# Prompt attention with unscaled probabilities and a token-major value product

## The chip, the cores and the metric

The kernel runs on one core of one Trainium2 chip. The time is that of one execution on the device in microseconds, the median of three runs. The core has five engines with their own instruction queues: TensorE (PE), the vector engine (DVE), ScalarE (ACT), GpSimd (POOL) and SyncE (SP, which here only starts DMAs). They wait for each other with semaphores.

## The reference

One inference step of a decoder layer for a prompt of 512 tokens and 8 sample tokens that each look back on 2048 cached ones. The part that the change touches:

```python
# group A, prompt: 8 heads, causal
s = (q_nope . k_nope + q_rope . k_rope) * MLA_SCALE;  p = softmax(s);  o_mla = p @ v
# group B, prompt: 8 heads, 2 key/value heads; the top-k (128) tokens of an indexer are kept
s = q . k * DSA_SCALE + rel_bias[t5_bucket(distance)];  p = softmax(masked s);  o_dsa = p @ v
# then, for prompt and sample tokens
mix = concat([rms_norm(o_mla, g_a), rms_norm(o_dsa, g_b)], axis=-1)     # each over its 512 columns
x = x + gate_m * (mix @ w_out)
# then norm, SwiGLU feed-forward network, gate, residual
```

All of it is in 32-bit floats.

## The kernel before, in words

Each engine has one program, written out in the order in which it runs. The list `AT` has 64 heads: group A then group B, in each the four query tiles of 128 tokens (`qt` 0 to 3), in each 8 heads. Query tile `qt` sees (qt + 1) x 128 keys, so a head is 128, 256, 384 or 512 keys wide.

**Attention loop.** One turn `u` per head:
- PE (lines 848 to 875): the scores of head u + 1 into `psV` (L854, waits until DVE has freed the slot), on odd turns the total of a count over partitions (L857, for the token search), the transposes of the probabilities of head u - 1, one per block of 128 keys (L864, waits for `p_ready`), and the value product of head u - 2 (L874). In that product the values are the weights (64 columns) and the transposed probabilities move (128 columns); the result is head dimension x tokens, two heads stacked.
- DVE (lines 1752 to 1785): in group A one instruction adds the causal mask and takes the row maximum (L1761), one scales the maximum (L1764). In group B first L1768 and L1769 scale the scores and add the position bias (`toepv`), then L1773 adds the mask (`msk`) and takes the maximum, L1774 negates it. Then, for the head before, the reciprocal of the sum of exponentials (L1778) and the scaling of the probabilities (L1779). Then one or two rounds of the prompt's top-k (`top_rounds`, 48 rounds: L1692, L1693) until they are done, which is at the end of group A, and one half step of the binary search for the sample tokens' top-k (`search`, 32 steps of two halves: L1717 to L1719, then L1722 and L1723 with the total from PE; after the sixteenth bit six more instructions).
- ACT (lines 1307 to 1326): exponentials with their row sum (L1314), copy of the transposed probabilities (L1321), every second turn copy of the value product into `mixT` (L1326).
- POOL: starts the fetch of cached rows by indirect DMAs.

After the loop DVE finishes the search (L1733 to L1748) and builds tables for the sample part.

**Sample part, group A** (`pe_decode`, `act_decode`, `dve_decode`): 8 samples x 16 pages (`m` = 16 b + j). Per page PE expands the cached latent rows (L913, 12 matmuls), every second page it transposes the next two pages (L896); ACT squares (L1345), DVE sums (L1808, L1809). At fixed `j` there are extra steps: transposes of the rope rows (L923, j = 1), and the weighing of the values of sample b - 1 (L943, j = 7), after which POOL starts the fetch of sample b + 1. The fetch of sample 0 of the other cache (`kv_rows_of(0, 0)`) is started before this part, into `qiz`.

**Group norm** (`pe_tail`, `act_tail`, `dve_tail`): squares of all of `mixT` on ACT (L1427), sums over partitions on PE with a matrix of ones (L1060), root (L1430), reciprocal (L1923) and scaling (L1925) on DVE, for group A and then for group B; then the split in a high and a low part (L1916, L1918) and the output projection (L1071). It begins when the last sample's result is in `mixT` (L1895).

## Time and profile before

| what | value |
|---|---|
| median of three runs | 1429.11 us (1425.79 to 1432.36) |
| profiled execution | 1427.2 us, span 1425.4 us |
| PE busy | 1258.9 us (88%) |
| DVE busy | 735.8 us (52%) |
| ACT busy | 406.5 us (29%) |
| POOL busy | 59.1 us (4%) |
| attention heads | 321.9 to 520.7 us of the span |
| sample part, group A | 530.4 to about 782 us |
| group norm before the projection | 909.4 to 938.1 us |

A row of a stretch has: from and to, length, then busy us and instructions of PE, PE weight loads, DVE, ACT and POOL, the granted PE clock as a share of 2.4 GHz, the share of the DMA engines, GB/s. A row of a timeline has: start in us of the span, length in us (from the first start to the last end of the instructions merged in it), engine, line, operation, output <- inputs, shapes, how many; in brackets the engine's idle time before it and what ended it. A 32-bit matmul leaves two PE records, a transpose one. A row by line has: busy us, mean ns of one, and the idle time before.

### The profile page before, as it was taken

Reading aid. Unit: us, or ns where it says so; the run is one execution under the profiler, and the core shown is the slowest. Engines: PE = TensorE matmul, PEld = TensorE weight load, DVE = VectorE, ACT = ScalarE, POOL = GpSimd, SP = SyncE. Lnnn points to the kernel's source line nnn. Section 1 sums busy time; section 2 is a strip of 40 time slices with the busy share of each in tenths; the row PEclk is TensorE's granted clock in tenths of the full one; section 3 lists DMA queues with packets and bytes.
Section 4 is the critical chain, followed back from the end, with each engine's and each line's share of the span. In section 5 each row is a group of like instructions: output and inputs, shape, how many; then the busy total and the mean of one; then the engine's idle time right before and its main releaser. Section 6 shows DMA issues by size and latency. Waiting matters only on the chain.

```text
span 1425.4 us, 22313 instructions
## 1 busy us (share of the span) xinstructions
PE 1258.9 (88%) x8981; PEld 1060.2 (74%) x8981; DVE 735.8 (52%) x1687; ACT 406.5 (29%) x782; POOL 59.1 (4%) x83
## 2 busy tenths in 40 slices
PE   6799999886987879999997996788699999988997
PEld 4688974543555559999997434587599999988997
DVE  1636727318998976656665102263633333347430
ACT  3323335332334535555555131201211101000001
POOL 2000020010000000000000001000000000000000
PEclk9899999995578989999999797889799999999999
DMA  9686620230001030122211654312133333332321
GB/s 316 160 251 187 195 67 1 60 89 1 0 1 67 1 128 1 68 74 111 85 67 60 195 226 189 121 45 74 31 89 92 99 88 88 88 96 62 102 81 60
DMA packets 138531, 135.98 MB, mean 95 GB/s; under 512 B 18222, under 2 KB 132283, under 8 KB 135668
## 3 DMA queue, kind: packets, MB, share of 16 engines
q1 hardware_dynamic: 133668, 83.29, 20.1%
q0 software_dynamic: 4784, 51.60, 9.6%
q8 instruction: 54, 0.88, 0.3%
q14 instruction: 25, 0.20, 0.0%
HBM read 131.40 MB, written 3.47 MB: 95 GB/s over the span
## 4 chain that ended last, share of the span: by engine, by line
PE 64%; DVE 22%; DMA 6%; issue 4%; ACT 3%; SPq 0%; POOL 0%; DVEq 0%; ACTq 0%; POOLq 0%
PE psV L1071 20%; PE psV L913 9%; PE psA L1071 9%; PE psA L662 6%; PE psV L1010 2%; DVE msk L1693 2%; DVE top L1692 2%; DVE r L1779 2%; PE psV L618 1%; DMA wide<-cache_mla,rows_of 1%; PE psA L1002 1%; PE psV L724 1%; PE psA L896 1%; DMA wide<-cache_kv,rows_of 1%; PE psV L1041 1%
## 5 line engine op out<-in xcount | busy, mean ns | idle before, releaser
L913 PE MATMUL psV<-r_r,wide_r 128*128 128x260 f32 x1536 | 201.8, 287 | 8.8 <-DVE wide_r L1802 7.7
L913 PEld LDWEIGHTS psV<-r_r,wide_r 128*128 128x128 f32 x1536 | 190.0, 190 | 10.4 <-issue 7.9
L1071 PE MATMUL psV<-qiz_r,wring_r 128*128 128x260 f32 x688 | 124.8, 285 | 0.0
L1345 ACT ACTIVATE wring<-psV 128x512 f32<-128x512 f32 x128 | 76.4, 597 | 93.5 <-PE psV L913 93.5
L1071 PEld LDWEIGHTS psV<-qiz_r,wring_r 128*128 128x128 f32 x688 | 101.4, 191 | 0.0
L1809 DVE TENSOR_REDUCE msk<-wring 128x8 f32<-128x512 f32 x128 | 86.4, 676 | 0.0
L662 PE MATMUL psA<-wide_r,wring_r 128*128 128x260 f32 x432 | 79.9, 289 | 6.4 <-DVE hT_r L2010 6.4
L1964 DVE TENSOR_TENSOR wide<-wide,psV 128x520 f32 (+1 forms) x22 | 15.3, 696 | 134.5 <-PE psV L1071 134.5
L1071 PE MATMUL psA<-qiz_r,r_r 128*128 128x260 f32 x352 | 71.8, 286 | 13.1 <-DVE hT_r L1918 13.1
L1071 PE MATMUL psA<-hT_r,r_r 128*128 128x260 f32 x352 | 71.9, 286 | 0.0
L1071 PE MATMUL psA<-qiz_r,wring_r 128*128 128x260 f32 x352 | 71.3, 284 | 0.0
L662 PEld LDWEIGHTS psA<-wide_r,wring_r 128*128 128x128 f32 x432 | 63.8, 192 | 7.7 <-issue 5.4
L1071 PE MATMUL psV<-qiz_r,r_r 128*128 128x260 f32 x272 | 57.0, 292 | 11.6 <-DVE hT_r L1918 11.6
L864 PE MATMUL psA<-mats,r 128*128 128x128 f32 x160 | 36.8, 336 | 33.7 <-DVE r L1779 33.4
L1071 PEld LDWEIGHTS psA<-qiz_r,r_r 128*128 128x128 f32 x352 | 55.0, 191 | 13.1 <-issue 13.1
L864 PEld LDWEIGHTS psA<-mats,r 128*128 128x128 f32 x160 | 22.2, 174 | 54.2 <-issue 54.1
L1904 DVE TENSOR_TENSOR wring_r<-wring,r_r 128x1024 fp32r<-128x1024 f32 (+1 forms) x47 | 60.8, 1294 | 1.6
L1071 PE MATMUL psV<-hT_r,r_r 128*128 128x260 f32 x272 | 56.7, 291 | 0.0
L1808 DVE COPY msk<-psV 128x8 f32<-128x8 f32 x128 | 21.1, 165 | 67.6 <-ACT wring L1345 67.0
L1071 PEld LDWEIGHTS psA<-qiz_r,wring_r 128*128 128x128 f32 x352 | 55.3, 192 | 0.0
L1071 PEld LDWEIGHTS psA<-hT_r,r_r 128*128 128x128 f32 x352 | 55.3, 192 | 0.0
L1314 ACT ACTIVATE r<-r,stat 128x128 f32<-128x128 f32 (+3 forms) x64 | 35.9, 561 | 67.5 <-DVE stat L1764 47.4
(457 smaller groups left out, 2533.5 us busy)
## 6 DMA issues: line engine op xcount, KB each, us to landing
wring<-w_ffn_in SPq DMA_DIRECT2D x44, 512.0 KB, 3.8
wide<-w_ada SPq DMA_DIRECT2D x11, 1024.0 KB, 6.7
wring<-w_ffn_out SPq DMA_DIRECT2D x16, 704.0 KB, 4.6
tok<-w_ada SPq DMA_DIRECT2D x9, 1024.0 KB, 8.0
wring<-w_in SPq DMA_DIRECT2D x24, 256.0 KB, 3.5
wring<-w_out SPq DMA_DIRECT2D x8, 512.0 KB, 4.4
wring<-w_in SPq DMA_DIRECT2D x20, 128.0 KB, 2.6
hT<-x_prompt SPq DMA_DIRECT2D x4, 512.0 KB
```

The source lines that it names most:

```text
L662: mm = pe.matmul(sa(n)[:, hf, 0:HT], w[:, kk, :], x[:, kk, hf * HT:(hf + 1) * HT], start=(kk == 0 and w is high and x is hT_hi), stop=(kk ...
L864: mm = pe.transpose(sa(n)[:, 0, kt * 128:(kt + 1) * 128], sP[:, (u - 1) % 3, kt * 128:(kt + 1) * 128], ident)
L913: mm = pe.matmul(kx[m % 2][:, hf, :], w, wtab[:, b % 2, l, 2 * k + hf, :], start=(k == 0 and w is high and l == 0), stop=(k == 1 and w is ...
L1010: mm = pe.matmul(sv(n)[0:64, c4 % 2, :], qdz[:, b * 64:(b + 1) * 64], kdT[:, c4 % 2, :], start=(b == 0), stop=(b == 7), skip_group_check=True)
L1071: mm = pe.matmul(out[:, hf, 0:HT], w[:, k, :], x[:, hf * HT:(hf + 1) * HT], start=(k0 + k == 0 and x is xh and w is high), stop=(k0 + k == ...
L1314: A(sP[:, u % 3, 0:W], sS[:, u % 3, 0:W], ACT.Exp, scale=(MLA_SCALE if g == 0 else 1.0), bias=stat[:, u % 3, 1:2], accum_out=stat[:, u % 3 ...
L1345: A(sq2[m % 2].rearrange("p (x n) -> p x n", x=2), kx[m % 2][:, :, 0:256], ACT.Square).then_inc(kx_squared, 1)
L1692: link(v.max(top8[:], msk[:, m0:m1]))
L1693: link(v.match_replace(msk[:, m0:m1], top8[:], msk[:, m0:m1], TAKEN))
L1779: v.tensor_scalar(sP[:, c, 0:W], sP[:, c, 0:W], stat[:, c, 3:4], None, ALU.mult).then_inc(p_ready, 1)
L1809: v.tensor_reduce(sums[b % 2][:, j, :], heads(sq2[m % 2]), AXX, ALU.add).then_inc(page_sums, 1)
L1904: v.tensor_tensor(low, raw, high.bitcast(F32), ALU.subtract).then_inc(w_split, 1)
```

## The change

- **Unscaled probabilities.** Scales and signs are folded into earlier gains (`gback`, `gT`), so the scores come negated and scaled; masks and biases are negated too. DVE does one instruction per head: add bias and take the minimum. ACT takes that minimum as it is, with scale -1, and writes the row sum into `lsum`. The scaling of the probabilities, their reciprocals and the scaling of the maximum are gone.
- **Token-major value product.** The transposed probabilities are the weights (128 columns), the values move (64 columns); 8 heads of a query tile stand side by side in one bank. Once per 8 heads DVE does `take_group`: reciprocal of the 8 sums, product of the 128x512 bank with them, into `otm` (in `qiz`). ACT's copies of the value product are gone; it squares each group once with a row sum (`square_mix`).
- **Bias and mask of group B** are added to each other on POOL (`combine`), into two buffers.
- **Group norm of the prompt.** Root and reciprocal once for all eight groups, at the start of the sample part. In its first four samples, twice each: ACT scales a group (`scale_mix`), PE transposes it (`mix_turn`, into the bank of the rope rows), DVE multiplies by the gain into `mixT` (`mix_take`). The norm at the end is left for the 8 sample tokens.
- The first fetch of `kv_rows_of` moves from before the sample part to its fifth sample (`b == 4`), behind the fetch for the seventh. One pad matmul (L1096) falls away, since the count of PSUM turns is now even.
- The top-k rounds stay where they are, at the same turns.

```diff
@@ pe_program, attention loop
-                    pe.wait_ge(p_ready, u)
+                    pe.wait_ge(exp_done, u)
...
-                    pair, p0 = (u - 2) // 2, (h % 2) * 64
+                    group = (u - 2) // 8
                     pe.wait_ge(a_free, A_PT + u - 1)
-                    if pair >= 2 and h % 2 == 0:
-                        pe.wait_ge(o_free, pair - 1)
+                    if group >= 2 and h == 0:
+                        pe.wait_ge(o_free, group - 1)
...
-                        mm = pe.matmul(psV[p0:p0 + 64, pair % 2, 1, 0:128], vv, sPT[:, (u - 2) % 3, kt * 128:(kt + 1) * 128],
+                        mm = pe.matmul(psV[:, group % 2, 1, h * 64:(h + 1) * 64], sPT[:, (u - 2) % 3, kt * 128:(kt + 1) * 128], vv,
                                        start=(kt == 0), stop=(kt == qt), skip_group_check=True)
@@ pe_decode
+            def mix_turn(x, b):
+                pe.wait_ge(mix_scaled, x + 1)
+                pe.wait_ge(kr_taken, b + 1)
+                if x >= 1:
+                    pe.wait_ge(mix_taken, x)
+                for c in range(4):
+                    mm = pe.transpose(krps[:, c * 128:(c + 1) * 128], otm[x][:, c * 128:(c + 1) * 128], ident)
+                mm.then_inc(mix_turned, 1)
...
+                if b < 4 and j in (9, 13):
+                    mix_turn(2 * b + j // 13, b)
@@ pe_tail
-            for g in range(2):
-                n = A_MIX + g
-                pe.wait_ge(sq2_written, 4 * g + 4)
...
+                for k in range(4):
+                    mm = pe.matmul(sa(n)[:, 0, g * 8:g * 8 + 8], ones, sqs[:, 4 * g + k, :], start=(k == 0), stop=(k == 3), skip_group_check=True)
@@ act_program, attention loop
-                    act.wait_ge(stats_ready, u + 1)
+                    act.wait_ge(v_free, V_S + u + 1)
...
+                if u >= 12 and u % 8 == 4:
+                    square_mix(u // 8 - 1)
+            square_mix(7)
@@ act_decode
+            act.wait_ge(o_squared, 8)
+            A(ss8, ss8, ACT.Sqrt, scale=1.0 / 512, bias=epsc[:]).then_inc(mix_root, 1)
...
+                if b < 4 and j in (5, 9):
+                    if b == 0 and j == 5:
+                        act.wait_ge(mix_rec, 1)
+                    scale_mix(2 * b + j // 9)
@@ dve_program
+            def take_group(x):
+                v.wait_ge(exp_done, 8 * x + 8)
+                v.reciprocal(rsum, lsum[x % 2]).then_inc(l_free, 1)
+                v.wait_ge(l_free, x + 1)
+                v.wait_ge(pv_done, 8 * x + 8)
+                v.tensor_tensor(heads(otm[x]), heads(psV[:, x % 2, 1, :]), rsum.unsqueeze(2).broadcast_to([128, H, 64]), ALU.mult).then_inc(o_free, 1)
...
+                if g == 0:
+                    bias = cext[:, 512 - W:512]
+                else:
+                    v.wait_ge(comb_ready, u - NA // 2 + 1)
+                    bias = comb[u % 2][:, 0:W]
+                v.tensor_tensor_reduce(sS[:, c, 0:W], sv(n)[:, 0, 0:W], bias, 1.0, -TAKEN, ALU.add, ALU.min, stat[:, c, 0:1]).then_inc(v_free, 1)
                 for _ in range(2 if u % 2 or u == 0 else 1):
                     next(rounds, None)
+                if u >= 8 and u % 8 == 3:
+                    take_group(u // 8 - 1)
+                next(steps)
+            take_group(7)
@@ dve_decode
+            v.wait_ge(mix_root, 1)
+            v.reciprocal(ss8, ss8).then_inc(mix_rec, 1)
...
+                if b < 4 and j in (10, 14):
+                    mix_take(2 * b + j // 14)
@@ pool_program
+            def combine(x):
...
+                if x >= 2:
+                    g.wait_ge(v_free, V_S + len(AT) // 2 + x - 1)
+                mask = cext[:, 384:512] if qt == 0 else msk[:, MQ[qt][0]:MQ[qt][1]]
+                if W > near:
+                    g.tensor_scalar(c[:, 0:W - near], mask[:, 0:W - near], toepv[:, h, 0:1], None, ALU.add)
+                g.tensor_tensor(c[:, W - near:W], mask[:, W - near:W], toepv[:, h, 256 - near:256], ALU.add).then_inc(comb_ready, 1)
...
+                if b == 4:
+                    g.wait_ge(mix_turned, 8)
+                    kv_rows_of(0, 0)
@@ sp_tail
-            sp.wait_ge(p_ready, len(AT))
+            sp.wait_ge(lat_pv, NB)
```

## Rows read from the trace of the kernel before

**Rows 1.** Busy time by engine, PE clock, DMA share, in four stretches.
```profile
321.90:390.00 68.10, 52.41 (x154) 31.59 (x155) 62.74 (x256) 21.10 (x69) 0.00 (x0) 0.50 0.00 1
390.00:439.60 49.60, 38.64 (x165) 24.36 (x163) 46.57 (x145) 17.22 (x42) 0.94 (x1) 0.79 0.13 48
439.60:520.70 81.10, 69.39 (x353) 45.08 (x353) 69.83 (x295) 39.67 (x113) 0.94 (x1) 0.92 0.07 26
530.40:782.00 251.60, 243.08 (x2118) 232.20 (x2118) 158.58 (x391) 140.84 (x251) 18.13 (x30) 0.99 0.18 66
```

**Rows 2.** DVE timeline, group A head: start us, us, engine, line, operation.
```profile
378.15 0.15 DVE L1764 TENSOR_SCALAR stat<-stat 128x1 f32<-128x1 f32 x1
...
378.75 0.55 DVE L1692 MAX8 top<-msk 128x8 f32<-128x384 f32 x1
```

**Rows 3.** DVE by line, 321 to 530 us: busy us, mean ns | idle before.
```profile
L1779 DVE TENSOR_SCALAR r<-r,stat 128x128 f32<-128x128 f32 (+3 forms) x64 | 24.8, 387 | 2.3
...
L1769 DVE SCALAR_TENSOR_TENSOR r<-psV,wring 128x256 f32<-128x256 f32 (+1 forms) x32 | 12.4, 388 | 0.8
...
L1768 DVE TENSOR_SCALAR r<-psV,wring 128x128 f32<-128x128 f32 (+1 forms) x16 | 6.6, 413 | 0.3
...
L1722 DVE TENSOR_SCALAR wring<-psA 128x8 f32<-128x8 f32 x32 | 5.2, 163 | 3.5 <-PE psA L857 2.9
```

**Rows 4.** The same view in the sample part: a 128x512 product from PSUM.
```profile
L1802 DVE TENSOR_TENSOR wide_r<-psA,wide_r 128x512 fp32r<-128x512 f32 x64 | 43.7, 684 | 21.9 <-ACT wide_r L1339 21.9
```

**Rows 5.** PE timeline, 512-key heads: full clock, then one at half clock.
```profile
503.39 1.13 PE L854 MATMUL psV<-kT,wide 128*128 128x512 f32 x2
504.35 0.28 PE L857 MATMUL psA<-wring,mats 128*128 128x8 f32 x2
504.92 0.63 PE L864 MATMUL psA<-mats,r 128*128 128x128 f32 x4 [0.28 <-DVE r L1779]
505.48 1.09 PE L874 MATMUL psV<-r,tok 128*64 128x128 f32 x8
506.50 1.12 PE L854 MATMUL psV<-kT,wide 128*128 128x512 f32 x2
...
416.21 1.97 PE L874 MATMUL psV<-r 128*64 128x128 f32 x8
418.11 2.08 PE L854 MATMUL psV<-wide 96*128 96x512 f32 x2
```

**Rows 6.** PE timeline: wide weights, few moving columns.
```profile
319.49 1.73 PE L844 MATMUL psV<-wz,r 128*128 128x16 f32 x14 [1.51 <-DVE small L1680]
```

**Rows 7.** POOL timeline: the same copy alone and beside DVE.
```profile
521.90 0.62 POOL L2063 COPY wide<-wide 128x512 f32<-128x512 f32 x1
535.73 1.40 POOL L2063 COPY wide<-wide 128x512 f32<-128x512 f32 x1 [13.22 <-PE psA L923]
```

**Rows 8.** DVE timeline at the end of group B.
```profile
517.48 0.29 DVE L1733 TENSOR_TENSOR wring<-wring 128x136 f32<-128x136 f32 x1
...
521.26 0.17 DVE L1738 COPY wring<-psA 128x8 f32<-128x8 f32 x1 [2.62 <-PE psA L879]
```

**Rows 9.** Chain that ended last, PE timeline, chain: transposes and fetches.
```profile
590.46 0.44 PE psA L896 x4
...
618.40 0.66 PE L896 MATMUL psA<-mats,wide 128*128 128x128 f32 x4 [0.61 <-DMA wide<-cache_mla,rows_of]
...
877.71 10.88 DMA wide<-cache_kv,rows_of
```

**Rows 10.** Timeline of all engines, group norm ahead of the projection.
```profile
909.36 4.32 ACT L1427 ACTIVATE r<-hT 128x520 f32<-128x520 f32 x8 [0.84 <-DVE hT L1895]
911.63 9.59 PE L1060 MATMUL psA<-r,mats 128*128 128x260 f32 x32 [3.37 <-ACT r L1427]
...
918.47 3.40 DVE L1923 RECIPROCAL r<-r 128x520 f32<-128x520 f32 x1 [9.21 <-ACT r L1430]
...
938.14 0.80 PE L1071 MATMUL psV<-qiz_r,r_r 128*128 128x260 f32 x2 [4.34 <-DVE hT_r L1918]
```

176 lines of the change are left out of this document (90 added, 86 removed).

## The prediction

> **What bounds the kernel now.** I read the stretches first, then the vector engine's (DVE) and TensorE's (PE) timelines inside each, then the waits. Four stretches matter. The heads of group A (latent attention) take 117.7 us (321.9 to 439.6) and the heads of group B (sparse attention) 81.1 us (439.6 to 520.7); DVE is busy for 109.3 and 69.8 of these [rows 1]. The rest is issue time of some 30 ns after each instruction; the only line that waits for PE is the one that reads a total, 2.9 us in all [rows 3]. DVE sets the pace of both. PE is not idle beside it: 91.1 and 69.4 us busy, and in 321.9 to 390 at a granted clock of 0.50, that is 1.2 GHz throughout [rows 1]. So it stands close behind. The third stretch, 520.7 to 530.4, is the end of the token search on DVE. The fourth, the sample part over the cached pages, has PE busy for 243 of 251.6 us [rows 1]: PE-bound, so what is added to PE there is paid in full. The last is the group norm ahead of the output projection, 909.4 to 938.1 us, a serial chain with PE mostly waiting [rows 10]. After it nothing is touched.
>
> **Group A, per head.** Removed from DVE: scaling of the maximum, reciprocal, and scaling of the probabilities. In a head of 384 keys that is from 378.15 to 378.75, 0.60 us [rows 2]. That head is a little wider than the mean of 320 keys; with the last of the three, the scaling, at 0.387 over all heads [rows 3] I take 0.56 per head, 17.9 us for 32. Added: once per eight heads one reciprocal (0.15) and one 128x512 product out of PSUM (0.68, as in the row of that shape [rows 4]), some 0.9 with its waits; three of them fall in group A: 2.7. DVE alone would give 15.2 us back.
> What is late next is PE. A head of 512 keys costs it 0.96 (scores), 0.56 (four transposes) and 1.02 (value product) at full clock, 2.54, or 0.635 per block of 128 keys. At half clock (1.2 GHz) the product takes 1.90, a factor of 1.86 [rows 5]. With half a total (0.15) a 512-key head is 2.7 at full and 4.9 at half clock. DVE now needs 117.7/32 = 3.7 per head on average. The stretch from 390 to 439.6 holds eleven wide heads, 4.5 each with one long search step of 2, so 4.3 without it and 3.7 after. So at full clock PE hides behind DVE; in a stretch at half clock the wide heads run at PE's pace, 1.2 us slower each. The clock was half up to 390 and mixed afterwards (0.79) [rows 1]. Two or three heads of this kind are likely: 3 us (0 to 7). Net in A: -12.
>
> **Group B, per head.** The same 17.9, and also the two instructions that scale the scores and add the bias: 12.4 + 6.6 us in 48 instructions [rows 3] and 0.04 of issue for each, 20.9 together. DVE would lose 38.8 of 81.1 us. It can't all be had: PE needs 0.635 x 80 blocks = 50.8, sixteen totals at 0.3 = 4.8 [rows 5], and about 0.1 fixed in each of the 24 narrower heads = 2.4, so 58 us at full clock. To this I add 2 for the 128-key heads (ScalarE is busy 39.7 us over the 32 heads [rows 1], so about 1 in a narrow one, and waits twice), 3 for entering (DVE's long step at the sixteenth bit) and draining, and 4 for one spell at half clock: 67. Gain 14 (8 to 18). A wide head with a total took 3.1 (503.39 to 506.50 [rows 5]) and PE needs 2.85 of it, so the widest gain least.
> The **swapped value product** has the probabilities (128 columns) as weights and moves 64 columns instead of 128. Nearest row: 128-column weights with 16 moving columns, 14 records in 1.73 us, 0.12 each [rows 6], against 0.128 now (eight in 1.02) [rows 5]. I take it as costing the same, bounds 0.11 to 0.20 per record (nothing overlapped); at 0.20 group B's 160 records cost 11 us more.
> The Trainium skill, "TensorE: Matmul & The Clock Gate", section on LDWEIGHTS, says that loading weights takes a time set by their columns, not their rows. That rule speaks against a gain from the swap: twice the columns are loaded, and by it one record could not fall under an estimated 107 ns. The rows above agree with it, and by the rule as by the rows the sum stays as it is.
>
> **Bias and mask on GpSimd (POOL).** 32 combinations, one or two instructions each, double-buffered, off DVE and PE. The trace has only one-input copies on this engine: 128x512 took 0.62, and 1.40 beside a busy DVE [rows 7]. A 256-column add of two inputs should be about 0.6, a 512-key head 1.1; beside DVE 2.5 at most. PE's pace is 2.7, so I cost it at nothing, with a bound of 0.5 us per wide head, 8 in all. The first one waits behind the first page fetch (0.94), under DVE's long step.
> The Trainium skill, "GPSIMD Engine Reference", sections "Engine selection" and "Key points", gives two-input work at about half DVE's rate, and contention with DVE instructions of two SBUF inputs. The 0.62 against 1.40 agrees with the second; no row here has a two-input instruction. If its factor held on top of the 1.40, wide heads would come at 3 to 4 us. That is the slow rival below.
>
> **End of attention.** Now DVE's four closing search steps (517.48 to 518.6) run while PE finishes the last products, and DVE then waits 2.62 for PE [rows 8]. After, they stand behind the last group's product, which waits for the last value product: 0.7 + 1.2 us join the path. +2. The squares and the square root on ScalarE lie beside the search's end on DVE (to 530.4): nothing.
>
> **Sample part.** Eight times four transposes on PE. A set of four costs 0.44 in the running pipeline [rows 9], so 3.5. The ScalarE scaling (0.6) and the DVE product (0.68) lie in a stretch where DVE is busy 63% and ScalarE 56% [rows 1]; I allow 0.5. Where the fetch ended the wait (0.61 before 618.40 [rows 9]) the extra PE work fills the gap: -1. The first rows of the other cache move from 520.95 to behind the fetch of the seventh sample; a fetch among others took 10.88 [rows 9], and the seventh sample's now has no slack to speak of, so +1 (0 to 8). Sum +4 (2 to 12). The first wait of w_out's load was never the last one: nothing. Early edits (two small scalings, negated masks): 0.3.
>
> **Group norm.** Now: eight squares 4.3, PE 9.6 (partly beside), root, reciprocal 3.4, four products 2.8, splitting 3.6, and the second group again 9.7 later; PE starts its second half at 938.14 [rows 10]. After, only the 8 samples: square 0.3, sixteen small PE records 2.0 to 3.9, root and three small DVE steps 1.2, split 3.6. PE starts at about 909.4 + 8 = 917.4. Its first half takes 5.2 at half clock, the second split 3.6, so no gap: second half at 922.6, and then nearer to full clock, since PE has by then worked without a pause, where now the second half starts after a wait of 4.3. Gain 15.5 + 2 = 17.5 (14 to 19).
>
> **Sum.** -12 - 14 + 2 + 4 - 17.5 + 0.3 = -37. The profiled execution took 1427.2 us (span 1425.4), giving 1390; the median of the three runs is 1.9 higher, so I say **1392**. All good ends together give -48 (1381), the bad ones -20 (1409).
>
> **Rivals.**
> (1) The clock stays at half in half of group B and the wide heads of A. For: A's first 68 us ran so [rows 1]. Against: PE gets denser, and group B now, with PE 86% busy, was granted 0.92 [rows 1]. Price: B (58 + 104)/2 + 5 = 86 instead of 67, A 4 more: 1415. Chance 0.10.
> (2) The swapped product doesn't overlap its weight load (0.20 per record): +11, 1403. Chance 0.10.
> (3) The sample part takes the additions badly: each of the 8 sets stalls PE for 0.44 + 0.6 + 0.7, and the moved fetch delays the seventh sample by 8: +18, 1410. Chance 0.08.
> (4) The change doesn't do what it says: PE, not DVE, already paces the attention, so the heads give nothing back; the end and the sample part cost 6 and the norm gives 17.5: 1417. Against: DVE's gapless timeline. Chance 0.04.
> (5) Slower: POOL paces group B. At 1.40 per input and instruction, a head of two blocks or less costs 2.8 and a wider one 4.2, mean 3.5 x 32 = 112 instead of 67: 1437. It decides from (67 + 37)/32 = 3.25 us per combination. Against: the other copy of that shape took 0.62 [rows 7]. Chance 0.03.
> The forecast has 0.65. A measurement of this kernel can tell about 0.5%, 7 us. (1) to (4) are still faster by more; within it the time comes only where (1) or (4) meets (3), 0.03 taken from the three. Faster 0.94, same 0.03, slower 0.03. Range: 1380 to 1412, down to the good ends and up to include (2) and (3); outside are (1), (4), (5).
>
> **What would show it.** In group B the start-to-start time of 512-key heads should be near 2.7, with PE busy over 95% and DVE near half; if DVE still has no gaps there, the PE part is wrong. Product records of 0.12 to 0.13 at full clock. DVE heads in A 0.5 to 0.6 shorter. PE's waits in B should not name POOL; DVE naming POOL often means (5). Page sets of 16 in the sample part about 0.9 longer for the first four samples, and no wait on a fetch in the seventh. From the last sample copy to the first projection matmul about 8 us, and no pause between the halves. A half clock over most of B, or a fetch wait over 3 us, would break the number.

## The result, and the profile after

The changed kernel takes **1379.26 us** (median of 4 runs, 1371.23 to 1384.65) against 1430.73 before (4 runs, 1425.79 to 1434.45): a ratio of 0.964, 95% interval 0.958 to 0.970, so 51 us less where 37 to 39 were forecast. Its profiled execution took 1384.65 us (span 1382.9), the slowest of the four; against the 1427.2 of the profiled execution before it is 42.5 us shorter. Steps are compared between these two traces. The rest of the 51 us is scatter: this execution lies 5.4 above the median of its kernel, that of before 3.5 below the median of its own.

The first view is the table of stretches of the changed kernel, to be laid beside [rows 1] (stretch in us, its length, busy time and instructions of PE, weight loads, DVE, ScalarE, GpSimd, then the granted clock, the share of the DMA engines and GB/s). Group A is now 323.4 to 425.2, group B 435.3 to 491.2.

```profile
323.40:390.00 66.60, 55.01 (x190) 41.88 (x191) 62.20 (x227) 22.07 (x73) 0.00 (x0) 0.51 0.00 1
390.00:425.20 35.20, 35.20 (x126) 27.29 (x125) 30.66 (x86) 12.49 (x29) 0.94 (x1) 0.50 0.03 6
425.20:435.30 10.10, 2.60 (x17) 2.46 (x16) 0.05 (x1) 0.00 (x0) 0.52 (x2) 0.67 0.53 214
435.30:491.20 55.90, 54.90 (x340) 46.74 (x340) 38.23 (x153) 36.54 (x105) 32.36 (x49) 0.86 0.06 19
...
502.60:762.70 260.10, 251.05 (x2185) 238.45 (x2185) 164.90 (x401) 145.58 (x259) 18.89 (x32) 0.98 0.19 72
```

The reader is to see three things. Group B has lost 25 us and PE is busy for 54.9 of its 55.9: DVE, which set the pace before, is busy for 38. Group A still goes at DVE's pace until 390, and largely at PE's behind it, at half clock. And between the groups stands a stretch of 10.1 us in which DVE and ScalarE do nothing and PE works for 2.6. The timelines of GpSimd and DVE show whose it is (start, duration, engine, line, operation, in brackets the idle time before it and what ended it):

```profile
423.16 0.94 POOL L2079 DMA_INDIRECT wide<-cache_mla,rows_of  x1 [111.13 <-PE psV L866]
434.78 0.77 POOL L2102 TENSOR_TENSOR wring<-cext,wring 128x128 f32<-128x128 f32 x2 [10.69 <-issue]
...
435.35 0.29 DVE L1813 CUSTOM_DVE_ANT_0 r<-psV,wring 128x128 f32<-128x128 f32 x1 [10.10 <-POOL wring L2102]
```

The first combination of bias and mask began 10.7 us after the page fetch ahead of it had been issued, with no semaphore to wait for, and DVE stood still for it. Below, this delay is called the hold. Its 10.7 us are steady, DVE's 10.1 are not: in the six other traces with the hold (e4, e5, e6, e9, e10, e14) GpSimd shows 10.7 to 11.4 us and DVE stood still for 6.5 to 8.4, since the fetch had been issued earlier there (in e5 4.4 us before DVE was ready, here 2.1).

Heads of 512 keys in group B, PE's timeline, the counterpart of [rows 5]:

```profile
480.49 1.08 PE L866 MATMUL psV<-kT,wide 128*128 128x512 f32 x2
481.40 0.60 PE L876 MATMUL psA<-mats,r 128*128 128x128 f32 x4
481.84 1.00 PE L886 MATMUL psV<-tok,r 128*128 128x64 f32 x8
482.68 1.08 PE L866 MATMUL psV<-kT,wide 128*128 128x512 f32 x2
```

From start to start the scores take 0.91, the transposes 0.44, the product 0.84: 2.19 us a head, where [rows 5] gave 0.96, 0.56 and 1.02. The group norm, the counterpart of [rows 10]:

```profile
883.86 0.26 ACT L1463 ACTIVATE r<-hT 128x64 f32<-128x64 f32 x1 [0.78 <-DVE hT L1941]
...
884.17 3.58 PE L1084 MATMUL psA<-r,mats 128*128 128x8 f32 x16 [1.35 <-ACT r L1463]
887.79 0.27 ACT L1465 ACTIVATE r<-psA,epsc 128x16 f32<-128x16 f32 x1 [2.37 <-PE psA L1084]
...
888.90 1.25 DVE L1962 CAST qiz_r<-hT 128x2080 fp32r<-128x2080 f32 x1
...
892.65 0.56 PE L1095 MATMUL psV<-qiz_r,r_r 128*128 128x260 f32 x1 [4.90 <-DVE hT_r L1964]
```

The projection starts 8.8 us after the first square and its two halves run 48.5 us without a pause.

Where the 42.5 us went, from one landmark to the next in both traces:

| Part | before, us | after, us | difference | forecast |
|---|---|---|---|---|
| up to the first head | 321.94 | 323.37 | +1.4 | +0.3 |
| group A, until DVE is ready for B | 117.70 | 101.88 | -15.8 | -12 |
| DVE waits for the first combination | 0 | 10.10 | +10.1 | 0 |
| group B, to the end of the last product | 81.04 | 55.79 | -25.3 | -14 |
| end of the search | 9.75 | 11.46 | +1.7 | +2 |
| sample part, to the selection matmuls | 257.06 | 260.10 | +3.0 | +4 |
| from there to the norm | 121.87 | 121.16 | -0.7 | 0 |
| norm and projection's two turns | 74.62 | 57.34 | -17.3 | -17.5 |
| the rest | 441.42 | 441.70 | +0.3 | 0 |

Three steps went otherwise than forecast: the hold, group B and, less, group A. The first beginning moves by chance: in kernels with the same instructions up to there it lay between 320.9 and 326.7.

### The profile page after: what moved, and what is told of

Same layout as the page of the kernel before. It is cut to its first block, busy times and chain, and to the rows that moved or that the text cites. A ratio compares the mean times of both kernels' runs of the same rounds, so it can differ in the third digit from the quotient of the medians.

```text
span 1382.9 us, 22166 instructions
## 1 busy us (share of the span) xinstructions
PE 1243.4 (90%) x8995; PEld 1077.5 (78%) x8995; DVE 684.2 (49%) x1468; ACT 401.0 (29%) x766; POOL 89.7 (6%) x131
## 4 chain that ended last, share of the span: by engine, by line
PE 74%; DVE 12%; DMA 5%; issue 3%; ACT 3%; SPq 1%; POOL 0%; DVEq 0%; ACTq 0%; POOLq 0%
PE psV L1095 21%; PE psV L925 11%; PE psA L1095 9%; PE psA L674 6%; PE psV L866 3%; PE psV L886 3%; PE psV L1035 2%; PE psA L908 2%; PE psA L876 2%; PE psV L630 2%; DMA wide<-cache_kv,rows_of 2%; PE psA L1027 1%; PE psV L736 1%; PE psA L956 1%; PE psV L1066 1%
## 5 line engine op out<-in xcount | busy, mean ns | idle before, releaser
L1095 PE MATMUL psV<-qiz_r,r_r 128*128 128x260 f32 x272 | 55.8, 287 | 4.9 <-DVE hT_r L1964 4.9
L1838 DVE TENSOR_TENSOR wide_r<-psA,wide_r 128x512 fp32r<-128x512 f32 x64 | 43.8, 686 | 24.7 <-ACT wide_r L1368 24.2
L1844 DVE COPY msk<-psV 128x8 f32<-128x8 f32 x128 | 21.1, 165 | 62.7 <-ACT wring L1374 61.3
L1981 DVE SCALAR_TENSOR_TENSOR xT<-psV,modT,xT 128x260 f32 (+1 forms) x16 | 7.8, 488 | 86.9 <-PE psV L1095 86.9
```

Of the source, the lines that this page charges most:

```text
L1095: mm = pe.matmul(out[:, hf, 0:HT], w[:, k, :], x[:, hf * HT:(hf + 1) * HT], start=(k0 + k == 0 and x is xh and w is high), stop=(k0 + k == ...
L1838: v.tensor_tensor(llo[p % 2], lps[p % 2], lhi[p % 2].bitcast(F32), ALU.subtract).then_inc(lat_split, 1)
```

## The experiments

### What holds the first combination

Two placements and an early addition. The additions and copies that e2, e5, e6, e13 and e17 put in also have a semaphore of their own, for which GpSimd waits right behind them; it is left out of the cuts:

```diff
 # e1: the fetch behind the first two combinations
-mla_rows(0)
 for x in range(len(AT) // 2):
+    if x == 2:
+        mla_rows(0)
     combine(x)
 # e2: an addition at the first head of group A
+g.wait_ge(v_free, V_S + 1)
+g.tensor_tensor(comb[0][:, 0:128], cext[:, 384:512], toepv[:, 0, 128:256], ALU.add)
 # e3: the first two combinations there
+g.wait_ge(v_free, V_S + 1)
+combine(0); combine(1)
```

> The changed kernel with one thing moved: GpSimd's first fetch of cached pages stands behind the first two combinations instead of ahead of them; all else as in the changed kernel (1379 us median, 1384.7 profiled). In that kernel the first combination began 10.7 us after the fetch was issued and DVE stood still for 10.1 us. Theory 'fetch' (an addition of two tensors queued behind an indirect fetch waits until the fetch has landed): the first two combinations come at once, near 423.5, and the third now waits for the fetch, so that group B is held two heads later; DVE's gap shrinks from 10.1 to about 8, 1377 us. Theory 'first use' (the first two-tensor operation on GpSimd after hundreds of microseconds takes some 10 us to start, whatever stands ahead of it): the first combination still begins 10 us after its release, DVE's gap stays at 10, and the fetch itself comes 11 us later: 1379 us, no change.

> The changed kernel with one more two-tensor addition of 128x128 on GpSimd, at the first head of group A (about 325 us), when that engine has nothing to do; its result is overwritten later. The fetch stays ahead of the first combination. Theory 'first use': the long start is paid there, where no one waits, the first combination follows the fetch within 1 us, and DVE's gap of 10.1 us at the start of group B is gone: 10 us of that, and up to 2 more because TensorE doesn't fall idle, 1368 us. Theory 'fetch': the gap stays, 1379 us.

> The changed kernel with the first two combinations of bias and mask made at the first head of group A, long before they are needed, and the fetch and the other thirty as they were. Theory 'first use': as with the early addition, the gap of 10.1 us is gone: 1368 us. Theory 'fetch': the third combination waits for the fetch until 434.8, and DVE with it: gap about 8, 1377 us.

Measured: 1369.88, 1371.12 and 1369.75 us (4 runs each; ratios to before 0.9605, 0.9600, 0.9595, intervals 0.956 to 0.965). The hold is gone in all three. GpSimd's timeline of the first and of the second:

```profile
416.95 0.79 POOL L2102 TENSOR_TENSOR wring<-cext,wring 128x128 f32<-128x128 f32 x2 [105.72 <-PE psV L866]
417.91 1.19 POOL L2079 DMA_INDIRECT wide<-cache_mla,rows_of  x1 [0.17 <-issue]
422.05 0.41 POOL L2102 TENSOR_TENSOR wring<-cext,wring 128x128 f32<-128x128 f32 x1 [2.95 <-DVE stat L1813]
```

```profile
322.83 0.41 POOL L2106 TENSOR_TENSOR wring<-cext,wring 128x128 f32<-128x128 f32 x1 [11.45 <-DVE stat L1814]
417.40 1.19 POOL L2080 DMA_INDIRECT wide<-cache_mla,rows_of  x1 [94.17 <-PE psV L867]
418.62 0.78 POOL L2103 TENSOR_TENSOR wring<-cext,wring 128x128 f32<-128x128 f32 x2
```

Neither theory stands. "Fetch" falls, since an addition behind the fetch runs at once (418.62, and 422.05 when DVE released it). "First use" in its plain form falls too: in the first kernel the first addition of all began 0.1 us after the score that released it. Only a first addition that stands behind the fetch had been held. The next two asked whether the kind of operation matters: a copy between fetch and combination, and a copy at the first head of group A.

```diff
 # e5
 mla_rows(0)
+g.tensor_copy(comb[0][:, 0:128], cext[:, 384:512])
 # e6
+g.wait_ge(v_free, V_S + 1)
+g.tensor_copy(comb[0][:, 0:128], cext[:, 384:512])
```

> The changed kernel with one plain copy of 128x128 on GpSimd between the first fetch of cached pages and the first combination. An addition made 94 us before the fetch, or just ahead of it, had removed the 10.7 us hold, and without a fetch ahead the first addition started within 0.3 us; so what is held is the first addition when the fetch is ahead of it. Theory 'kind' (it is the first use of this kind of operation that is held while the fetch moves its data): the copy runs within 1 us of the fetch, and the combination behind it still comes 10 to 11 us after the fetch. Theory 'any' (the first tensor operation of any kind behind the fetch is held, for instance because the engine has to be brought back from issuing fetches): the copy itself comes 10 to 11 us after the fetch and the combination right behind it. Time near 1379 in both.

> The changed kernel with one plain copy of 128x128 on GpSimd at the first head of group A, where the earlier experiment had an addition. Theory 'kind': a copy doesn't prepare an addition, the first combination is held for 10.7 us behind the fetch as in the changed kernel, about 1379 us. Theory 'any': the early copy does the same as the early addition, no hold, about 1370 us.

```profile
419.04 0.94 POOL L2080 DMA_INDIRECT wide<-cache_mla,rows_of  x1 [105.90 <-PE psV L867]
419.98 0.29 POOL L2107 COPY wring<-cext 128x128 f32<-128x128 f32 x1
430.94 0.77 POOL L2103 TENSOR_TENSOR wring<-cext,wring 128x128 f32<-128x128 f32 x2 [10.66 <-issue]
```

```profile
323.42 0.29 POOL L2106 COPY wring<-cext 128x128 f32<-128x128 f32 x1 [11.39 <-DVE stat L1814]
417.63 0.97 POOL L2080 DMA_INDIRECT wide<-cache_mla,rows_of  x1 [93.92 <-PE psV L867]
430.03 0.77 POOL L2103 TENSOR_TENSOR wring<-cext,wring 128x128 f32<-128x128 f32 x2 [11.43 <-issue]
```

Theory "kind" holds: the copy runs at once and prepares nothing (1378.07 and 1379.86 us, one run each). That is also why the copy of [rows 7] had told nothing. But not every new kind is held: the other instruction of a combination first ran in the changed kernel at 456.62, behind 16 additions, and started when DVE released it (its 0.72 us are 0.12 more than the later ones of that size took):

```profile
456.62 0.72 POOL L2101 TENSOR_SCALAR wring<-msk,wring 128x128 f32<-128x128 f32 x1 [0.68 <-DVE stat L1813]
```

Last, the first addition behind a short fetch, and behind plain DMA issues, where no fetch is near:

```diff
 # e13: behind the last index-page fetch
+g.tensor_tensor(comb[0][:, 0:128], cext[:, 384:512], toepv[:, 0, 128:256], ALU.add)
 # e17: behind the fifteen plain issues
+g.tensor_tensor(warmt[:], tok[:, 4, 0:16], tok[:, 4, 16:32], ALU.add)
```

> The changed kernel with one addition of 128x128 on GpSimd directly behind the last of the eight index-page fetches (near 311 us), which is shorter than the page fetch that held the first combination: it lands about 4 us after its issue, the page fetch 9.4 to 9.6 us. Theory 'landing' (the first addition behind a fetch waits until the fetch's data have landed): the addition starts 3 to 5 us after that fetch's issue. Theory 'fixed' (a fixed time of some 10.7 us): it starts 10.7 us after. Theory 'only there' (no hold behind this fetch): within 1 us. In all three the later hold at the first combination should be gone, since an addition has been made before: total about 1370.

> The changed kernel with one small addition (128x16) on GpSimd right behind its fifteen plain DMA issues, near 208 us, with no indirect fetch ahead of it, no wait in front of it and nothing that needs the engine for the next 65 us. So far the first addition on this engine was held 8.4 us behind a short indirect fetch and 10.7 to 11.4 us behind a long one, and not at all where the engine had waited for a semaphore right before it. Theory 'preparation' (the first addition needs some 8 us before it runs, whatever stands ahead, and a wait in front of it hides them): it starts about 8 us after the last issue. Theory 'indirect fetch' (only an indirect fetch ahead holds it): it starts within 0.5 us. In both the hold ahead of group B should be gone, since an addition has been made: about 1370 us.

```profile
311.86 0.94 POOL L2080 DMA_INDIRECT r<-cache_idx,rows_of  x1 [3.07 <-PE psA L846]
321.22 0.40 POOL L2089 TENSOR_TENSOR wring<-cext,wring 128x128 f32<-128x128 f32 x1 [8.42 <-issue]
```

```profile
213.82 0.21 POOL L2077 TENSOR_TENSOR warmt<-tok 128x16 f32<-128x16 f32 x1 [7.00 <-issue]
```

The first addition on GpSimd starts 7.0 us late with no indirect fetch ahead of it, only the plain issues ("preparation"), 8.4 behind a short fetch, 10.7 to 11.4 behind a long one, and with nothing that shows if the engine has stood at a semaphore right ahead of it (11 us in the second kernel, 106 in the first). Later additions never waited. In each held case a DMA issue stood ahead of the addition, at most with a copy between; a first addition with no issue ahead and no wait was not run. "Landing" falls (8.4 us behind a fetch that lands in about 4). Why a fetch lengthens it was not tried.

The Trainium skill, "GPSIMD Engine Reference", section "Instruction dispatch", tells of a first call to a freshly loaded kernel that pays some 6 us of loading "with no visible profile instruction". The trace agrees in kind (idle time put down to "issue"), and differs in size, 7.0 to 11.4. That code is loaded here is not shown: in the changed kernel, e5, e13 and e17 no packet of the two instruction queues that the profile lists falls into the hold (in the changed kernel, with its hold from 424.1 to 434.8, the nearest begin at 415.0 and 445.1).

The last two kernels were at 1374.7 and 1374.9 us in their one run, not at the 1370 expected: in these executions group A took 102.3 and 102.6 us instead of 99.3, its last heads being at half clock.

All that was run without the hold and otherwise unchanged but for the place or number of additions (e1, e2, e3, e13, e17; 14 runs) has a median of 1370.3 us, what was run with it (the changed kernel, e5, e6; 6 runs) 1379.3. The 9 us between them fit the 6.5 to 10.1 for which DVE stood still. So one line moved gives the best version found. One of the changed kernel's four runs, 1371.23, lies among those without the hold; it left no trace, and why stays open.

### What paces group B, and what the turned product is worth

```diff
 # e4: every value product of group B made twice
-for kt in range(qt + 1):
+for kt in list(range(qt + 1)) * (1 if g == 0 else 2):
 # e10 (added, seven heads of eight), e14 and e18 (instead; e18 with the fetch moved as in e1)
+pe.matmul(psV[0:64, group % 2, 1, c0:c0 + 128], vv, sPT[...kt...], start=(kt == 0), stop=(kt == qt))
```

> The changed kernel with every value product of group B made twice into the same place (160 more matmul records of 128 weight columns and 64 moving columns, the result the same). It prices one record of the turned product and shows what paces group B. If TensorE paces it, as forecast, the 55.9 us from the first head of group B to the last product grow by 160 records: by 16.8 at 0.105 us (as in the changed kernel's trace at full clock), by 20.5 at the 0.128 that the prediction took, by 32 at 0.20 (weight load not overlapped). If DVE or GpSimd pace it, it grows by less than 5. Total about 1379 + 18 = 1397.

> The changed kernel with a value product of the old orientation (64 weight columns, 128 moving columns) added to that of the new one in seven of eight heads of group B: 140 more records; they are written over by the product that counts, so the result is the same. The kernel with the new product made twice (128 weight columns, 64 moving) had 160 more records and was 17.1 us longer from the first head of group B to the last product (72.9 against 55.8 us), 0.107 each. Theory 'the swap costs nothing and gains nothing' (both orientations 0.107 in a full pipeline): 140 x 0.107 = 15.0, so 70.8 us. Theory 'the old one is dearer' (0.128, as its eight records in 1.02 us were read before): 140 x 0.128 = 17.9, so 73.7 us. If half of the moving columns is what counts in full (0.21): 85 us. Total about 1394.

> The changed kernel with the value product of group B put back to the old orientation (64 weight columns, 128 moving columns, 160 records as before); group A keeps the new one. Its results of group B land transposed and partly on each other, so the attention outputs of that group are wrong in content; the work of every engine is the same in amount. Group B from its ninth-last block on is read at full clock: in the changed kernel a head of 512 keys costs TensorE 0.91 + 0.44 + 0.84 = 2.19 us. Theory 'the swap gains': the old orientation costs 0.92 + 0.56 + 1.02 = 2.50 as in the kernel before and in the kernel with the old product added, 0.31 us more per head of 512 keys, 0.078 per block of 128 keys, 6.2 us over group B's 80 blocks (55.8 becomes 62). Theory 'equal': 55.8 within 1 us, and the old price was high only because the queue had pauses.

> The kernel with the fetch behind the first two combinations (1369.9 us, group B in 53.3 us), with the value product of group B in its old orientation (64 weight columns, 128 moving); the attention outputs of that group are wrong in content, the work is the same in amount. With the hold the old orientation made group B 68.1 us long instead of 55.8: 12.3 us, where 0.31 us per head of 512 keys at full clock give 6.2. Theory 'product and clock': without the hold TensorE has no long pause ahead of group B and leaves the half clock sooner, so that the difference is 6 to 9 us: group B 60 to 62 us, total 1376 to 1379. Theory 'product alone': the difference is 12 us here too, group B 65 us, total 1382.

Group B, from its first reduction on DVE to the end of the last product. The times of e4, e10 and e14 are single runs, and the trace of e18 is of the slowest of its four (1390.79):

| Kernel | whole, us | last 16 heads (384, 512 keys) | first 16 heads | time, us |
|---|---|---|---|---|
| changed | 55.8 | 32.8 | 23.0 | 1379.3 |
| fetch moved (e1) | 53.3 | 32.8 | 20.6 | 1369.9 |
| product twice (e4) | 72.9 | 46.6 | 26.4 | 1392.5 |
| old one added (e10) | 82.9 | 49.7 | 33.2 | 1405.7 |
| old one instead (e14) | 68.1 | 38.4 | 29.7 | 1396.4 |
| the same without hold (e18) | 70.1 | 38.4 | 31.7 | 1382.3 |

PE paces the group: 160 more records cost 17.1 us, 0.107 each. That is a mean: in the wide heads they were paid in full (112 records, 13.8 us; a head of 512 keys went from 2.19 to 3.09, 0.112 a record), in the narrow ones 48 cost 3.4, so there PE sets the pace for a part of the time only. The Trainium skill, "TensorE: Matmul & The Clock Gate", section on LDWEIGHTS, gives an estimated 107 ns for loading 128 columns; the 0.112 of the trace is near it. And the **swap is no exchange of equals**. With the old orientation back, a head of 512 keys takes 2.51 us at full clock instead of 2.19, in PE's timeline of e14:

```profile
488.70 1.13 PE L866 MATMUL psV<-kT,wide 128*128 128x512 f32 x2
489.66 0.60 PE L876 MATMUL psA<-mats,r 128*128 128x128 f32 x4
490.19 1.09 PE L887 MATMUL psV<-r,tok 128*64 128x128 f32 x8
491.21 1.13 PE L866 MATMUL psV<-kT,wide 128*128 128x512 f32 x2
```

The product is 1.02 instead of 0.84 from its start to that of the next kind, the transposes ahead of it 0.53 instead of 0.44, the scores 0.96 instead of 0.91. Yet inside the product the old records follow each other at 0.109 us and the new ones at 0.112. What the old orientation pays for are the changes of kind: from the last transpose to the first product 0.20 (new: 0.11), from the first product to the second 0.16 (0.06), from the last product to the scores 0.20 (0.11), and 0.05 inside the scores. The rows of the weight loads (PEld) show the same, first in e14, then in the changed kernel:

```profile
490.19 0.85 PEld L887 LDWEIGHTS psV<-r,tok 128*64 128x64 f32 x8 [0.17 <-issue]
491.21 0.30 PEld L866 LDWEIGHTS psV<-kT,wide 128*128 128x128 f32 x2 [0.17 <-issue]
```

```profile
481.73 0.97 PEld L886 LDWEIGHTS psV<-tok,r 128*128 128x128 f32 x8
482.62 0.30 PEld L866 LDWEIGHTS psV<-kT,wide 128*128 128x128 f32 x2
```

In the old orientation the first load of each new kind begins only with its own matmul (490.19), 0.17 us after the load before it has ended; in the new one it begins 0.11 ahead of it (481.73 and 481.84) and without a gap. Whether the 64 weight columns or the 128 moving ones are the cause was not separated.

Over the last 16 heads the old orientation costs 5.6 us in both kernels (e14 and e18), a step that repeats to 0.01 us. The narrow heads lose 6.7 more in e14, where PE was granted 0.50 from 425 to 455 us, for the first 23 us of the group (15 in the changed kernel). Without the hold the whole difference to e1 did not shrink as "product and clock" expected: 16.7 us between the traces (clock 0.50 up to 450 in this execution, the slowest of its four; in that of e1 half clock for 3.4 us of the group) and 12.4 in the medians (1382.26, 4 runs 1376.82 to 1390.79), as "product alone" had it. How much of it belongs to the clock alone stays open; 5.6 us at full clock is the part that is shown.

The added product (e10) cost 27.1 us, more than every theory but the last: beside half clock in the narrow heads, at full clock it made the transposes 0.53 and the new product 0.94, so that a head grew from 2.19 to 3.40 us, by more than its own 1.02: with one more kind in the head there are more changes to pay for. Prices per record taken alone don't add up where kinds alternate.

### GpSimd or DVE for the combinations

```diff
-v.wait_ge(comb_ready, u - NA // 2 + 1)
+if W > near: v.tensor_scalar(bias[:, 0:W - near], mask[:, 0:W - near], toepv[:, h, 0:1], None, ALU.add)
+v.tensor_tensor(bias[:, W - near:W], mask[:, W - near:W], toepv[:, h, 256 - near:256], ALU.add)
```

> The changed kernel with the combinations of bias and mask made by DVE itself in each head of group B, GpSimd doing only the fetch. No hold behind the fetch, so it compares with the kernel that has the fetch behind the first two combinations (1369.9 us). Theory 'TensorE paces group B with room on DVE': DVE is busy for 38 of 56 us there; 32 additions of 128 to 256 columns and 16 of one input, some 0.25 to 0.4 us each, add 12 to 15 us of work to DVE, most of it into its gaps; heads of 512 keys stay near 2.2 us, narrow ones become 0.3 us longer: 1370 to 1378 us. Theory 'DVE is close behind': the additions are paid in full, 12 to 15 us: 1383.

1378.19 us (4 runs, ratio 0.964, interval 0.960 to 0.967); group B 59.7 us against 53.3. So GpSimd's help is worth about 6 us in the group (2.7 of them in the last 16 heads, at full clock in both; in the first 16 this execution also stood at half clock for 8 us, that of e1 for 3.4) and 8.3 in the medians. In the changed kernel the hold takes it back: without GpSimd at all it would run as fast. DVE's timeline of this kernel, above, and GpSimd's of the changed one, below, for a head of 512 keys:

```profile
468.37 0.35 DVE L1816 TENSOR_SCALAR wring<-msk,wring 128x256 f32<-128x256 f32 x1
468.76 0.43 DVE L1817 TENSOR_TENSOR wring<-msk,wring 128x256 f32<-128x256 f32 x1
```

```profile
482.40 0.92 POOL L2101 TENSOR_SCALAR wring<-msk,wring 128x256 f32<-128x256 f32 x1
483.29 0.64 POOL L2102 TENSOR_TENSOR wring<-msk,wring 128x256 f32<-128x256 f32 x1
```

1.56 us on GpSimd and 0.78 on DVE, beside PE's 2.19.

### The other parts

Three of the four transposes of each turned output left out (`range(1)` for `range(4)`), and the norm for the samples alone in the kernel before (its tail's three places taken from the change):

> The changed kernel with three of the four transposes of each of the eight attention outputs left out (24 of 32 left out; only the first 128 of each 512 columns are turned, so the attention outputs that go on are incomplete; this leaves work out). It prices what the turns cost on TensorE in the sample part, which runs from the first expansion matmul to the first of the 32 selection matmuls: 257.1 us before, 260.1 in the changed kernel, and between 259.1 and 260.1 in four of its variants. If the turns are paid in full on TensorE (four in 0.44 us, as in the prediction), the part shortens by 8 x 0.33 = 2.6 us, to about 257. If they lie in gaps that DVE, ScalarE or the page fetches leave, it shortens by less than 1. Total 1377 by the first.

> The kernel before with one part of the change alone: the group norm ahead of the output projection done only for the eight sample columns, as in the changed kernel. The norm of the 512 prompt tokens is left out (in the change it is done in the attention), so the output is incomplete. Theory 'the norm is a gain of its own': 17.3 us off, as between the traces of before and of the changed kernel (74.6 to 57.3 us from the last sample copy to the end of the second half of the projection): 1428.9 - 17.3 = 1411.6. Rival 'part of it comes with the attention' (weights loaded earlier, another clock): 8 to 12 us only, 1418.

The sample part took 257.1 us with a quarter of the transposes (1375.02 in one run): 2.0 to 3.0 less than in the changed kernel and its first variants, where 2.6 were expected if PE pays them in full: so it does. The norm alone gave 1410.53 us (4 runs, ratio 0.986, interval 0.984 to 0.989), 18.7 us off its own runs of before: a gain of its own.

The closing steps of the search ahead of the last group's product (a `yield` ahead of their wait, one `next(steps)` ahead of `take_group(7)`, fetch moved):

> The kernel with the fetch behind the first two combinations (1369.9 us), and in addition the first four closing instructions of the token search (two comparisons, two sums over 128x136) ahead of the last group's product on DVE instead of behind it. In the changed kernel DVE waits 2.7 us for the last value product, then makes the group's product (0.69) and the four closing steps (1.2), and only then TensorE can add up. Theory: those 1.2 us, and the 0.7 of the group's product that then runs beside TensorE's totals, leave the path: 1.5 us, 1368.4. Rival: what follows waits for something else (the page fetch or ScalarE), 1369.9. The difference is at the edge of what the timing can tell, so it is read from the time between the last value product and the first expansion matmul, 11.4 us in the changed kernel.

From the last product to the first expansion 9.6 us instead of 11.9 in e1; in the time (1371.53, 4 runs) it doesn't show above the spread.

### The clock in group A

```diff
 # e7: value products of group A repeated (128, 256, 384, 512 keys)
-for kt in range(qt + 1):
+for kt in list(range(qt + 1)) * ((14, 7, 4, 3)[qt] if g == 0 else 1):
 # e12: scores repeated; e15: the same without the 17
+for _ in range(0 if g == 1 else 17 if u == 0 else (5, 3, 1, 0)[qt]):
+    pe.matmul(sv(n)[:, 0, 0:W], lhs, rhs, start=True, stop=True)
```

> The changed kernel with the fetch behind the first two combinations (1369.9 us), and TensorE filled up in group A: the value product of a head of 128, 256, 384 or 512 keys is made 14, 7, 4 or 3 times into the same place, so that TensorE has about as much work per head at full clock as DVE. In the changed kernel the granted clock falls to 0.50 with the first head of group A and stays there for 80 to 100 us; the wide heads then come at TensorE's pace. Theory 'idleness' (the clock falls since TensorE is half idle beside the narrow heads): the clock stays near 1.0, the wide heads come at DVE's pace of 3.0 to 3.7 us instead of up to 4.9, and group A ends 5 to 10 us earlier: 1362. Theory 'granted anyway' (the clock falls whatever TensorE does there): the fill costs double, 11 to 20 us more in the wide heads and some in the narrow ones: 1390 to 1400.

> The kernel with the fetch behind the first two combinations (1369.9 us), and TensorE filled up in group A with repeated score matmuls (up to 512 moving columns each) where the earlier fill repeated value products (64 moving columns, and mostly weight loads): the score of a head of 128, 256, 384 or 512 keys made 6, 4, 2 or 1 times, and that of the second head 18 times, in the 5.3 us in which DVE prepares the search and TensorE was idle. In the earlier fill the clock stood at 0.50 for 170 us although TensorE was never idle. Theory 'moving columns' (what holds the clock up is matmuls that move many columns, not busy time): the clock stays near 1.0 through group A, whose wide heads then come at DVE's pace, and it ends 4 to 8 us earlier: 1362 to 1366. Theory 'idle gap' (it is the 3 us without any matmul at the start that lets it fall): the same result, and the fall would be gone from the first heads on. Theory 'not by filling': the clock is at 0.50 all the same and the fill costs up to 48 us: 1400 to 1418.

> The kernel with repeated scores in group A (clock 1.00 from 330 to 360 us, 0.81 to 400), but without the 17 repeated scores in the first 5.3 us of the group, so that TensorE is idle for 3 us there again. Theory 'gap': the clock falls to 0.50 at that gap and stays there through the first 30 us and more, as in the changed kernel, in spite of the repeated scores, and these cost: the narrow heads go from 2.25 to 3 us and more, the group becomes 10 to 40 us longer. Theory 'columns': it falls at the gap and comes back within a few heads, since the repeated scores move enough columns: the group takes 100 to 104 us as with the first fill.

Times: 1482.77 (4 runs, ratio 1.037), 1371.89 (4 runs), 1371.21 (one). The first is far above both expectations, the second 6 us and more above the 1362 to 1366 of "moving columns". The stretch from 360 to 380 us of the changed kernel and of the kernel with repeated products, then 340 to 360 us of the one with repeated scores and no fill at the start:

```profile
360.00:380.00 20.00, 19.80 (x67) 14.53 (x67) 18.76 (x63) 6.48 (x19) 0.00 (x0) 0.50 0.00 0
```

```profile
360.00:380.00 20.00, 20.00 (x92) 19.53 (x92) 6.58 (x26) 2.39 (x9) 0.00 (x0) 0.50 0.00 1
```

```profile
340.00:360.00 20.00, 18.30 (x105) 15.42 (x105) 18.66 (x73) 6.48 (x24) 0.00 (x0) 1.00 0.00 1
```

With repeated products PE was never idle from 340 to 505 us and was granted 0.50 (1.2 GHz) all the while; with repeated scores 1.00 (2.4 GHz) from 330 to at least 360, with a fill at the start or without one, so "gap" and "idleness" fall. After 372 us with the fill at the start and 389 without it the clock fell here too (0.81 as the mean from 360 to 380 with it), so the higher level was not kept through the wide heads. What the chip goes by is not settled. It would bring little here: group A took 100.3 and 101.4 us with repeated scores and 99.3 in e1, which stood at half clock up to 411. Its heads up to the 24th come at DVE's pace at either level; only the last four or five gain, 2.6 us between the traces of the changed kernel (half clock to the end of the group) and of e1.

## Why the prediction was right or wrong

**Direction and parts** were right: norm 17.3 for 17.5, sample part 3.0 for 4, end 1.7 for 2; the early edits and w_out's load cost nothing to be seen. For the moved fetch I gave 1 us. The seventh sample's own landed in 9.2 us, the moved one behind it in 13.6, the eighth's in 10.1, and PE waited for the eighth's once, for 0.30; the seventh sample took 31.2 instead of 30.7: half a microsecond. The time, 1379.3, fell 0.7 us below the range and 13 below the forecast. Of the 13, 5.4 lie between the traces (42.5 for 37.2) and 7.3 in the scatter: I had put the median 1.9 above the trace, and it lies 5.4 below it. So that the time fell below the range and not inside it is chance; that the parts missed by 4, 10 and 11 us is not. One sum is wrong too: the bad ends as stated (gains of 8 in A, 8 in B and 14 at the norm, costs of 12 in the sample part and 2 at the end) add up to -16 (1413), not to -20 (1409).

**Group B, the failed step: "I take it as costing the same".** The swapped product was priced at nothing (its bound of 0.11 would have been a gain, and was not used). The runs put at least 5.6 us on it, and 12 to 17 with the clock of those runs. My 67 us were indeed near what the old orientation takes, 68.1 and 70.1. Record by record the two do cost the same, 0.109 and 0.112 in a row of their kind. But my 0.128 was eight records and the changes around them divided by eight, and the 0.56 for the transposes holds such a change too. The swap took 0.33 us of changes out of each head of 512 keys, and I had left them in. The 0.12 of [rows 6] was read from the first start to the last end; from start to start those records are 0.112 apart. The estimate from the Trainium skill, 107 ns for one record, stood beside it and was near what was measured; it says nothing of the changes, and I had read it as speaking against a gain only. At 2.19 us for four blocks the swap makes 80 x (0.635 - 0.548) = 7 of the 67. The other 7 down to the 53.3 of e1 are allowances: of 9 us for narrow heads, entry and draining, and half clock, e1 used 2.3, and the changed kernel 2.5 more for the clock (23.0 against 20.6 in the first 16 heads, with 15.2 against 3.4 us at half clock).

**GpSimd, the second failed step: "The first one waits behind the first page fetch (0.94), under DVE's long step. I cost it at nothing."** The queue order was right, the price was not: 10.1 us in this trace, 6.5 to 8.4 in others, 9 in the medians. The trace of before has no addition on GpSimd, and I bounded its running time, not its start; rival (5) looked at the pace, which was 1.56 a head of 512 keys where I had said 1.1 and at most 2.5, never the bound. Two errors of opposite sign met: without the hold the forecast would have been 22 us off. That it missed by 13 only is luck.

**Group A, a term too small.** Eight heads took 25.6, 26.9, 30.7 and 34.5 us before and 21.4, 22.6, 25.8 and 32.1 after. With 0.9 for each of three group products and 2.6 for the clock the removal is 21.1 us, 0.66 a head, where I had taken 0.56 from [rows 2, 3] (17.9 us); it goes from 0.53 in the first eight heads, where no group product is made, to 0.73 in those of 384 keys. The clock's 3 us (0 to 7) were 2.6 in this execution and nothing in e1; the group products' 2.7 were right.

**Rivals.** (1) came in a part of its condition and not in its price: half clock held for all of A but for only 15 of the 56 us of B, and cost 2.6 and 2.5 us, since DVE is the slower one in A and only the narrow heads of B were hit. (2) falls by the records (0.112). (5) falls too: the 24 additions of 128x256 took 0.64 us each beside a DVE that was 68% busy, and DVE waited for GpSimd only in the hold. (3) falls, the sample part grew by 3.0 and PE waited 0.30 for a fetch. (4) falls with group B. Of the signs, PE's share held (98% of group B) and so did the projection's (8.8 us, no pause); the head of 512 keys (2.19 for "near 2.7"), the product records and the heads of A did not, and the four samples with turns grew by 2.0, 0.5, 0.1 and 0.5 us, not by 0.9 each. The changed kernel's runs spread over 13 us. In the traces of its variants the first head began between 320.9 and 326.7 us, group A took 99.3 to 102.6 without the hold, and group B 53.3 to 57.0 with the same instructions, so no one place makes the spread.

## What to carry to other kernels

Before giving an idle engine a kind of instruction that it has not run yet, let it run one such instruction early, where nothing waits for it: on GpSimd the first addition was held for 7 to 11 us, and DVE stood still for up to 10.1 of them, more than the 6 that the help brought in the group. Which operand is the weight and which one moves is a price of its own, and here it lay in the changes between kinds and not in the records: read the start-to-start time of a whole head, with its neighbours, and not of one record. And when an engine's pace is removed, the next engine's allowances decide the number; add them only where a row shows them.

## What was not expected of the hardware

- The first two-input addition on GpSimd starts 7.0 us late behind plain DMA issues, 8.4 behind a short indirect fetch, 10.7 to 11.4 behind a long one; the time is booked as "issue". Copies, memsets and fetches before it don't take it away; where the engine had stood at a semaphore right ahead of it (11 us and more) none showed.
- On GpSimd adding a per-partition scalar to 128x256 took 0.92 to 1.04 us, longer than adding two tensors of that size, 0.64; on DVE it is 0.35 and 0.43.
- PE was granted half its clock for 165 us without an idle moment when it repeated products of 128 weight and 64 moving columns.
- At full clock records of 128 weight and 64 moving columns follow each other at 0.112 us, those of 64 weight and 128 moving columns at 0.109; but between transposes and scores with 128 weight columns eight of the first kind took 0.84 us and eight of the second 1.02, and with the neighbours the head 2.19 and 2.51.
